# Transposes before values in the software pipeline of a prompt attention (one core)

## The reference

```python
logits = einsum('nbqgrd,nbkgd->nbgrqk', qb, kb) * ATT_SCALE + bias
probs  = masked_softmax(logits, mask)
out    = einsum('nbgrqk,nbkgd->nbqgrd', probs, vb)
```

## Time and profile before

| | |
|---|---|
| time, median of 3 runs | 2564.99 us (2563.7 to 2567.42) |
| the profiled execution, its own time | 2563.7 us |
| its span | 2561.9 us |
| PE busy | 2266.9 us, 88% of the span |
| DVE / ACT / POOL busy | 971.8 / 577.1 / 473.2 us |
| mean granted TensorE clock | 0.943 of full |
| prompt attention, first product to last `finish` | 1121.3 to 1545.3 us of the span |

### The profile page before, as it was taken

How to read it: one execution, slowest core, us unless ns; L and a number is a source line. 1 busy time by engine, 2 the same in 40 slices (tenths; PEclk the granted TensorE clock), 3 DMA queues, 4 the chain that set the end, 5 groups by cost and what they waited for, 6 DMA issues and landing times. The chain is left out here.

```text
span 2561.9 us, 34788 instructions
## 1 busy us (share of the span) xinstructions
PE 2266.9 (88%) x13808; PEld 1470.0 (57%) x13808; DVE 971.8 (38%) x2332; ACT 577.1 (23%) x1255; POOL 473.2 (18%) x678
## 2 busy tenths in 40 slices
PE   7999989999594388648887888999999999999998
PEld 3445657656362266525555554478888888844443
DVE  3101003333131154325555552257776775600110
ACT  3000003333121134235555561111010111100100
POOL 1314212221200156200112221013223322100000
PEclk8999998999776699879999999999999999999999
DMA  7712106774834689632212413146665643420110
GB/s 243 206 72 79 44 37 246 287 279 157 263 120 178 169 349 413 221 119 83 66 47 69 138 32 107 66 156 203 207 228 184 230 136 96 147 84 1 60 36 17
DMA packets 166328, 376.19 MB, mean 147 GB/s; under 512 B 48199, under 2 KB 104975, under 8 KB 148368
## 3 DMA queue, kind: packets, MB, share of 16 engines
q1 hardware_dynamic: 131964, 148.68, 18.6%
q0 software_dynamic: 25728, 149.56, 15.3%
q10 hardware_dynamic: 8474, 75.73, 8.6%
HBM read 345.56 MB, written 99.65 MB: 174 GB/s over the span
## 5 line engine op out<-in xcount | busy, mean ns | idle before, releaser
L2610 PE MATMUL ff_ps<-ff_hx,ff_aw 128*128 128x264 f32 x2464 | 550.1, 386 | 0.9 <-DVE ff_hx L2849 0.9
L2610 PEld LDWEIGHTS ff_ps<-ff_hx,ff_aw 128*128 128x128 f32 x2464 | 467.4, 190 | 80.7 <-issue 1.2
L337 PE MATMUL in_ps<-in_w,in_xT 128*128 128x512 f32 (+1 forms) x512 | 199.6, 545 | 0.0
L754 ACT ACTIVATE pa_L<-pa_L,pa_nm 128x640 f32<-128x640 f32 (+3 forms) x192 | 141.7, 740 | 65.0 <-DVE pa_nm L790 64.7
L780 DVE CUSTOM_DVE_ANT_0 pa_L<-pa_psS,pa_T 128x512 f32<-128x512 f32 (+3 forms) x288 | 138.0, 529 | 48.1 <-PE pa_psS L638 48.1
L337 PEld LDWEIGHTS in_ps<-in_w,in_xT 128*128 128x128 f32 x512 | 95.3, 190 | 93.5 <-issue 84.9
L638 PE MATMUL pa_psS<-pa_kT,pa_qT 64*128 64x512 f32 (+3 forms) x576 | 119.8, 516 | 27.7 <-DVE pa_mx L780 27.4
L654 PE MATMUL pa_psT<-pa_ident,pa_L 128*128 128x128 f32 x816 | 118.0, 279 | 27.5 <-DVE pa_PT L806 15.9
L459 DVE TENSOR_SCALAR in_yout<-in_ps 128x512 f32<-128x512 f32 (+2 forms) x44 | 26.1, 593 | 300.3 <-PE in_ps L337 190.9
L672 PE MATMUL pa_psO<-pa_PT,pa_V 128*64 128x128 f32 x1632 | 112.0, 281 | 16.5 <-issue 10.9
L1024 DVE COPY cmp_KT<-cmp_psT 128x512 f32<-128x512 f32 x128 | 88.6, 692 | 97.4 <-PE cmp_psT L940 97.4
(11 more groups left out here) (380 smaller groups left out, 3066.6 us busy)
## 6 DMA issues: line engine op xcount, KB each, us to landing
out_new_a_k_s<-in_cache_a_k ACTq DMA_DIRECT2D x8, 4088.0 KB
out_new_a_v_s<-in_cache_a_v ACTq DMA_DIRECT2D x8, 4088.0 KB
ff_aw<-in_w_up SPq DMA_DIRECT2D x44, 512.0 KB
in_w<-in_w_in SPq DMA_DIRECT2D x5, 2048.0 KB
cd_X<-in_cache_a_k SPq DMA_DIRECT2D x8, 1024.0 KB
cd_X<-in_cache_a_v SPq DMA_DIRECT2D x8, 1024.0 KB
ff_hx<-in_w_down SPq DMA_DIRECT2D x14, 512.0 KB, 4.3
cd_X<-in_cache_a_k SPq DMA_DIRECT2D x24, 256.0 KB
```

The lines of the kernel that those rows point to most:

```text
L337: mm = pe.matmul(ps[0:n, b, 0:width], xT[:, k, t * P:t * P + n], w[:, ch % WBUF, k, 0:width], start=(k == 0), stop=(k == KC - 1))
L754: nc.scalar.activation(x, x, ACT.Exp, bias=nm[:, s, h:h + 1], scale=1.0, accum_out=sm[:, s, h:h + 1]).then_inc(s_ex, 1)
L2610: mm = pe.matmul(ps[:, bank_of(x, j, g), 0:H2], aw[:, j % 2, at, k, :], hx[:, bt, k, g * H2:g * H2 + H2], start=(k == 0), stop=(k == KH - 1))
```

## The change

On PE alone, the transposes of unit s-2 are issued before the values of unit s-3, where they came after them. Both keep their waits and instructions; nothing else in the program differs.

```diff
                     scores(s)
+                if 2 <= s < U + 2:
+                    transposes(s - 2)
                 if s >= 3:
                     values(s - 3)
-                if 2 <= s < U + 2:
-                    transposes(s - 2)
```

## The result

The change makes the kernel slower. Over 13 runs its median is 2583.35 us, that of the kernel before in the same jobs 2567.42 us; the ratio is 1.0058, with a 95% interval of 1.0045 to 1.0072. That is some 15 us, where I forecast 0.9 us less. The profiled execution of the changed kernel took 2585.95 us for a span of 2584.1.

What follows compares the result with a forecast made beforehand. A DVE and ACT ring was taken to bound the large units, PE and its copies the steps of units 1 to 3. Terms -2.3 + 0 + 2.0 - 0.55 = -0.85 us gave 2564.1 us against a median of 2565.0; range 2557 to 2573.

Steps and rivals of the forecast that it cites:

- DVE and ACT ring: Units 5 to 8: logits, exponentials, weight row, finish, next logits set the pace, 4.29 us in pass 10; PE has slack.
- the long one: Transposes' wait before unit 5's third bank in passes 2, 5 and 8: 2.79 us before, 3.9 us forecast.
- stall and clock: Passes 2, 5, 8: longer stall, values behind it at 1.2 GHz; 0.5 us each plus 0.5 for another stretch, +2.0 us.
- 20-bank passes: Eight passes with 20 banks of transposes: lateness in following small steps nets 0, bounds -0.5 and +1.0 us a pass.
- window passes: Behind passes 9, 10 and 11 values release the weight row earlier: 0.77 us gained each, -2.3 us.
- end of the stage: After unit 96: last transposes run before unit 95's values, which cover unit 96's copies; -0.55 us.
- The clock: Slower rival: low clock after every long transposes' wait, 1.36 us in each of eight passes, 10.9 us; 2573 us; chance 0.10.
- those three steps of a pass: Units 1 to 3 of the next pass: ring short, PE still on units 6 to 8, so time can move there.
- the lateness: Behind pass 3: weight row released 0.25 us late in unit 1's step, 0.58 in unit 2's, made up in unit 3's.
- Values gate the weight row: Slower rival: in steps of units 1 to 3 late values delay weight row and finish; 8.0 us, 2572 us; chance 0.17.
- the replay: Steps behind pass 10 re-timed in the new order with trace durations: weight row 0.59 us earlier, gain then 0.77 us, kept.
- my own bounds of both: Upper prices over eight 20-bank passes: late values 1.0 us each, 8.0 us; low clock 1.36 us each, 10.9 us.

Runs made afterwards that it cites:

- the filled kernel: Changed kernel with unread products (16, 8, 7 in passes 2, 5, 8; 8 or 5 in other 20-bank passes) filling the transposes' long stalls: stage 420.8 us, ratio 1.0014.

## Why the prediction was wrong

The reading of the stage held in part: a DVE and ACT ring paces the large units (4.29 4.77 5.25 5.73 in both kernels), the transposes' waits take the place of values' waits, the long one is 3.93 us where I had 3.9, and at full clock it costs nothing (6.62 and 7.52 us for the steps of units 7 and 8 in the filled kernel). The forecast of 2564.1 us was wrong in two terms. Term by term, with the changed kernel and the filled one to part them:

| term of the sum | forecast | measured | from |
|---|---|---|---|
| stall and clock | +2.0 | +9.4, some 7.9 of it new | 430.2 - 420.8; less 1.5 before |
| 20-bank passes | 0 | +6.9, some 8.3 at full clock | passes of the filled kernel, 303.7, against 296.9; and 1.5 more |
| window passes | -2.3 | -0.4 | 30.83 against 30.95 |
| end of the stage | -0.55 | -0.6 | 24.58 against 25.15 |

**The first step that failed is the clock's price**: "I price this at 0.5 us a pass, three passes 1.5, and 0.5 more for one stretch of low clock somewhere else that is not there now." In passes 5 and 8 the step of unit 8 lost 1.64 us (9.17 against 7.53), in pass 2 it lost 0.79, and low stretches came in the step of unit 1 behind passes 3, 6 and 7, where there had been none, at 1.1, 2.2 and 1.6 us against the same passes of the filled kernel. The time at low clock rose by 20.5 us. The rival "The clock" had the mechanism, but not its reach: it took 1.36 us in each of eight passes, 10.9 in all, and it was six passes at 0.8 to 2.2 us, 9.4 in all. I gave it 0.10. What I held against it, that behind the stall in pass 8 the scores ran at full pace, looked at too short a stretch: the clock fell in that pass too, only a step later, behind another wait of 2.15 us. This is 1 us of the kernel before:

```profile
1409.00:1410.00 1.00, 1.00 (x14) 1.00 (x12) 0.00 (x0) 1.00 (x3) 0.00 (x0) 0.50 0.00 0
```

The rule of the Trainium skill, "TensorE: Matmul & The Clock Gate", Part 1, that activity has to keep the clock up, was on the right side, and the filled stalls agree with it: with PE busy in them the low clock was gone.

**The second is where the new order can lose time at full clock**: "So only those three steps of a pass" (units 1 to 3) "and the places where the new order makes PE late for the ring, can move the time", and "in that of unit 3 the lateness is gone". These are the steps of the filled kernel less those of the kernel before, the latter from passes whose step had no low clock:

| pattern | unit 1 | unit 2 | unit 3 | unit 4 | pass |
|---|---|---|---|---|---|
| a | +0.12 | -0.35 | +0.46 | +0.56 | +0.8 |
| b | +0.70 | -0.35 | +0.17 | +0.61 | +1.1 |
| c | +0.47 | +0.62 | -0.39 | +0.62 | +1.3 |

Behind pass 3, the one that I replayed (c), unit 3's step makes up 0.39 of 1.09 us and 0.70 stay. And the step of unit 4, which my argument left out, loses some 0.6 us in each of the eight passes, 4.7 of the 8.3. There values and, behind them, the scores end late: the logits wait for scores 0.17, 0.38 and 0.45 us in the steps of units 2, 3 and 4 behind pass 4 of the changed kernel. In the steps of units 1 and 2 it is the weight row that waits for L678, as the rival "Values gate the weight row" says (22 times, 16.4 us, where it did so once). That rival had 1.0 us a pass, 8.0 in all, and a chance of 0.17. That the code waits for both heads' scores is not the reason: the first alone would be ready only 0.05 us earlier. In window passes the steps of units 1 and 2 came out near the replay (in pass 10 2.79 and 3.91 where I had 2.73 and 3.80); unit 3's took 3.45 instead of 2.98 and gave most of the gain back.

**Both slower rivals came true at once.** I priced them one at a time, so the range ended at 2573. With my own bounds of both, -2.3 + 8.0 + 10.9 - 0.55 is 16.1 us, and the stage lost 15.3. That the two agree so well is in part luck, since the window passes and the clock were each off, in opposite directions.

The Trainium skill, "TensorE: Matmul & The Clock Gate", "Why this matters for your kernels", says that products with few rows run concurrently when they lie in distinct row groups. The 0.05 us agree.

**A cost I had not listed** is switching: "It removes and adds no instruction" is true, but the old order had L678 and the block transposes side by side. In the changed kernel scores start 0.26 us after L678 (1282.27 to 1282.53), where transposes started 0.17 us after it. It is part of the lateness above, at 0.2 to 0.4 us a pass, some 4 us over twelve passes, and is shown by the two runs that moved L678; why PE takes longer there is not.

What stays open: why low stretches fall on some passes and not on others with the same instructions. No run here parts that, and the stage lengths are from one execution each, so how often a given pass falls to it isn't measured.

## What to carry to other kernels

In a pipeline written out by hand, ready work belongs inside the wait of the other work, not ahead of all of it or behind all of it. Here the two banks that can go went first, values filled the wait, and the rest followed; with a better choice of banks the stage fell from 414.9 to 391.2 us. Before moving an instruction on TensorE, list what stands behind each of its waits and how long PE will idle, since a stall that costs nothing by itself can halve the pace of the work behind it. Replay every step of a pass and ask in each what releases the first instruction of the next, here the scores as well as finish. And add up the rivals that can come true together before setting the upper end of a range.

## What the runs showed of the hardware

- Products of two heads, in the two halves of the array's rows, are issued one after the other in a group that takes 1.06 us. Logits that waited for the first head alone started only 0.05 us earlier behind the start of the group (1.26 against 1.31 us).
- A change between transposes and products on PE cost about 0.1 us (0.26 against 0.17 us from L678 to what follows), and 0.2 to 0.4 us a pass in both orders.
- A stretch at half clock in the step of unit 1 cost 1.6 us on the mean. It fell on some passes and not on others with the same instructions and waits (behind a wait of 1.79 us, and not behind one of 1.80). In the two profiles with the stalls filled by 0.22 us products nobody reads, there was none.
